# Two-block model kernel: unread matmuls added on TensorE in the attention stage, four at each pair of heads and twenty ahead of the first quarter turn

## The reference, cut to what matters

```python
q = rms_norm_2(q.reshape(b, t, N_HEADS, HEAD_DIM), q_gain)
k = rms_norm_2(k.reshape(b, t, N_KV_HEADS, HEAD_DIM), k_gain)
...
qx = apply_axial_rope(qx, ang_r, ang_c)
kx = apply_axial_rope(kx, ang_r, ang_c)
...
s_win = jnp.einsum('bkgqd,bkjd->bkgqj', qb, kb).astype(jnp.float32) * scale
s_win = jnp.where(valid, s_win, -jnp.inf)
s_ctx = jnp.einsum('bkgqd,bkcd->bkgqc', qb, kc_t).astype(jnp.float32) * scale
p = sink_softmax(jnp.concatenate([s_win, s_ctx], axis=-1), sink_g).astype(vb.dtype)
return (jnp.einsum('bkgqj,bkjd->bkgqd', p[..., :3 * BLOCK], vb)
        + jnp.einsum('bkgqc,bkcd->bkgqd', p[..., 3 * BLOCK:], vc_t))
```

## Time and profile before

| | before |
|---|---|
| median of 3 runs | 5205.73 us (5204.96 to 5208.75) |
| profiled execution, span | 5216.1 us |
| PE busy | 4445.1 us, 85% |
| DVE busy | 2553.7 us, 49% |
| ACT busy | 1587.3 us, 30% |
| POOL busy | 544.8 us, 10% |
| first DMA issue of attention to its last output's DMA issue | 3124.63 to 3447.36 us |

### The profile page before, as it was taken

How to read it: one execution, slowest core, us unless ns; L and a number is a source line. 1 busy time by engine, 2 the same in 40 slices (tenths; PEclk the granted TensorE clock), 3 DMA queues, 4 the chain that set the end, 5 groups by cost and what they waited for, 6 DMA issues and landing times. The chain is left out here.

```text
span 5216.1 us, 87974 instructions
## 1 busy us (share of the span) xinstructions
PE 4445.1 (85%) x38358; PEld 3430.0 (66%) x38358; DVE 2553.7 (49%) x3625; ACT 1587.3 (30%) x2492; POOL 544.8 (10%) x496
## 2 busy tenths in 40 slices
PE   7999968888887678786888786789999899687999
PEld 5888857777776456563222264467888787576787
DVE  4556666667775665542111224654443312575553
ACT  3222223333332453431000124433222211563332
POOL 0000021111110356000000002310000000000000
PEclk9999979999998789897999998889999999898999
DMA  6656710000000020422999731021122133112232
GB/s 243 228 192 216 273 59 22 15 14 14 14 6 31 25 69 17 167 84 99 420 421 421 291 103 36 18 100 53 61 65 71 62 112 123 67 60 79 85 100 94
DMA packets 165534, 604.11 MB, mean 116 GB/s; under 512 B 24032, under 2 KB 37216, under 8 KB 139808
## 3 DMA queue, kind: packets, MB, share of 16 engines
q1 hardware_dynamic: 151920, 538.72, 28.8%
q0 software_dynamic: 13232, 59.77, 2.9%
HBM read 526.97 MB, written 71.46 MB: 115 GB/s over the span
## 5 line engine op out<-in xcount | busy, mean ns | idle before, releaser
L1903 PE MATMUL f_acc<-f_a_lo,f_w_hi 128*128 128x512 f32 x4048 | 1037.0, 359 | 63.0 <-DVE f_a_lo L2125 29.0
L1903 PEld LDWEIGHTS f_acc<-f_a_lo,f_w_hi 128*128 128x128 f32 x4048 | 668.9, 190 | 189.0 <-issue 42.6
L1903 PE MATMUL f_acc<-f_a_lo,f_w_lo 128*128 128x512 f32 x2288 | 691.9, 358 | 0.0
L1892 DVE TENSOR_TENSOR f_w_lo<-f_w_raw,f_w_hi 128x1024 fp32r<-128x1024 f32 (+1 forms) x176 | 228.3, 1298 | 542.9 <-ACT f_w_hi L1887 542.9
L1903 PEld LDWEIGHTS f_acc<-f_a_lo,f_w_lo 128*128 128x128 f32 x2288 | 380.8, 190 | 66.2
L1887 ACT CAST f_w_hi<-f_w_raw 128x1024 fp32r<-128x1024 f32 (+1 forms) x176 | 194.7, 1106 | 613.8 <-DMA f_w_raw<-in_ffn_w_up 221.0
L1903 PE MATMUL i_acc<-i_x_hi,i_w_hi 128*128 128x512 f32 (+1 forms) x1024 | 308.4, 357 | 13.5 <-DVE i_x_lo L2680 10.0
L352 DVE COPY_PREDICATED rw_work<-rw_mask_x,rw_big 128x512 f32<-128x512 uint8 x288 | 238.7, 881 | 155.4 <-PE rw_big L642 150.2
L1903 PE MATMUL i_acc<-i_x_hi,i_w_lo 128*128 128x512 f32 (+1 forms) x1024 | 310.7, 359 | 0.0
L1903 PE MATMUL i_acc<-i_x_lo,i_w_hi 128*128 128x512 f32 (+1 forms) x1024 | 307.2, 356 | 0.0
L642 PE MATMUL rw_big<-rw_work,rw_halves 128*64 128x64 f32 x4608 | 260.8, 222 | 2.0 <-issue 1.9
(11 more groups left out here) (518 smaller groups left out, 8083.6 us busy)
## 6 DMA issues: line engine op xcount, KB each, us to landing
ex_w<-in_exp_w SPq DMA_DIRECT2D x192, 1024.0 KB, 16.6
i_mod_rows<-in_ada_rows SPq DMA_DIRECT2D x128, 512.0 KB, 4.7
f_w_raw<-in_ffn_w_up SPq DMA_DIRECT2D x88, 512.0 KB, 3.5
i_w_raw<-in_w_in_both SPq DMA_DIRECT2D x44, 512.0 KB, 3.6
f_w_raw<-in_ffn_w_down SPq DMA_DIRECT2D x32, 704.0 KB, 4.1
i_w_raw<-in_w_in_lat SPq DMA_DIRECT2D x40, 512.0 KB, 4.5
pt<-i_stage POOLq DMA_DIRECT2D x22, 768.0 KB, 6.0
f_w_raw<-in_hgrn_w_both SPq DMA_DIRECT2D x24, 512.0 KB, 3.6
```

The source lines that it names most:

```text
L1892: dve.tensor_tensor(self.view(self.w_lo, u), self.view(self.w_raw, u), self.view(self.w_hi, u).bitcast(F32), ALU.subtract).then_inc(self.r ...
L1903: op = pe.matmul(acc[:, a:b], part[:, k], xs[:, k0 + k, a:b], start=(first and k == 0 and part is w_hi and xs is x_hi), stop=(last and k = ...
```

## The change

Two things are added on PE, and two waits change places. `spin(count)` issues float32r products of the identity (`ident_r`) with the 384 columns of the window mask (`mask_r`) into `T_BANK`; nothing reads what they write, and the next set of transposes overwrites it. Ahead of the first set of each of the 48 pairs stand four of them, behind the waits for the copies of `T_BANK` and ahead of the wait for `scaled`, which now comes last. Ahead of group 0's quarter turn stand twenty, behind a wait for `consts_done` (DVE has made `ident_r` and `mask_r`) and ahead of the wait for `normed`. In all 212 matmuls are added. The other engines' programs are as they were.

```diff
+                def spin(count):
+                    for _ in range(count):
+                        pe.matmul(big[:, T_BANK, 0:3 * CH], ident_r[:], mask_r[:], start=True, stop=True)
+
                 def quarter_turn(s):
                     g = slots[s][1]
+                    if g == 0:
+                        pe.wait_ge(S["consts_done"], 1)
+                        spin(20)
                     pe.wait_ge(S["normed"], g + 1)
...
                     tiles = turns(b)[k]
-                    pe.wait_ge(S["scaled"], 2 * n + 1 + tiles[-1] // len(keys(b)))
                     if turned_until[n] + k:
                         by_dve, by_act = copies_until(n, k)
                         pe.wait_ge(S["pt_copied"], by_dve)
                         if by_act:
                             pe.wait_ge(S["pt_copied_act"], by_act)
+                    if k == 0:
+                        spin(4)
+                    pe.wait_ge(S["scaled"], 2 * n + 1 + tiles[-1] // len(keys(b)))
                     for q, tile in enumerate(tiles):
```

## The result

The changed kernel takes 5230.2 us in the median of 13 runs (5206.1 to 5237.9), the kernel before 5203.8 us in the median of 13 (5188.2 to 5209.2). The ratio is 1.0046, 95% interval 1.0035 to 1.0057: slower by 24 us, 18 to 30. The prediction was 5228, with 0.71 on slower.

What follows compares the result with a forecast made beforehand. PE was taken as the busiest engine in attention (76%), though not always busy. Exposed batches 26.1 + 2.3, less clock 5.6 and the twenty 0.3, gave +22.5 us: median 5228 us, 8-in-10 range 5209 to 5241.

Steps and rivals of the forecast that it cites:

- Price of four: Four added matmuls ahead of a pair's first set: 0.9 us at full clock (0.71 to 1.08), 1.65 at half clock.
- Exposed batches: 29 of 48 batches of four stand where nothing hides them: 26.1 us, plus 2.3 for half clock.
- b5: Last pair of a half group: its four are exposed, since its probabilities move along with the delay; 0.9 us each.
- b0's own batch: First pair of a half group: its four are covered by waits and idle time, cost nothing; 5 us more if uncovered.
- b2: Third pair in five half groups: four start after DVE's late copy, miss the 2.52 us gap, full price exposed.
- The clock that comes back: Half-clock loss regained through the added matmuls over the attention stage: 5.6 us of 24.8.
- b4 to b5 in the first halves: Fifth to sixth pair: four partly fill a 3.1 us gap, so half the lost clock returns, 3.2 us.
- b1 to b2: Second to third pair in first halves: half of the 2.8 us lost to the clock returns, 1.4 us.
- The first pair: Start of the stage: the 2.39 us gap holds the four with room to spare, 1.0 us of clock returns.
- All that the clock could give: Attention stage: total lost against full clock, the most that a restored clock could return, 24.8 us.
- Rival 1: Attention stage: 48 batches keep the clock full throughout, 26.1 - 24.8 = +1.3 us, so 5207; chance 0.17.
- The twenty: Ahead of the first quarter turn: they run in idle time and return 0.3 us; bounds 1.5 loss, 2.7 gain.

Runs made afterwards that it cites:

- the two kernels that take the places apart: Against the changed kernel, four matmuls kept only at the 29 pairs held exposed, or only at the other 19: ratios to before 1.0047 and 1.0011.
- the 15 batches on top of the filled gaps: Four matmuls added at the last three pairs of five half groups, against the kernel with gaps filled: attention 315.9 us from 306.7, ratio to before 1.0002.
- the filled gaps: Against the changed kernel, unread matmuls only where the trace of before has PE idle, in numbers sized to fill it: attention 306.7 us, ratio to before 0.9983.
- the one with the 29 alone: Against the changed kernel, the four kept only at the 29 pairs predicted to be exposed: attention 340.7 us, ratio to before 1.0047.
- the hidden places alone: Against the changed kernel, the four kept only at the 19 pairs predicted to be hidden: attention 319.6 us, ratio to before 1.0011.

## Why the prediction was right

**The side and the size.** 22.5 us were predicted; the ratio gives 24 (18 to 30) and the stage in the profile 19.4 to 22.0. The mechanism, that most waits for `scaled` are not waits and that the four are paid there, is shown by the two kernels that take the places apart and by the 15 batches on top of the filled gaps. Of the signs named beforehand some missed: from b3 to the next b0 11.85 us against 13.3 expected, the first turn 4.54 against 5.5, and one of the five b2 gaps was followed by full clock. One reading was wrong, though no term rests on it: a mean clock of 0.86 between 1.0 and 0.5 says that 0.28 x 290 = 81 us pass at half clock, and 41 us is what that costs against full clock.

**Price of four.** Predicted 0.9 us (0.71 to 1.08) and 1.65 at half clock; measured 0.81 and 1.45. The first float32r matmul of a batch costs more than the others: four take 0.81, eight 1.53, and forty take 7.21 where twenty take 3.74, so 0.174 for each further one. The estimate by the Trainium skill's page "TensorE: Matmul & The Clock Gate", section "Back-to-back issue gap" (0.65 us for four), came out too low, since here the first of a batch costs more; by the same formula one of 384 columns is estimated at 0.1625 us, near the 0.174 of a long run.

**Exposed batches.** Predicted 26.1 + 2.3 = 28.4 us for the 29; measured 18.0 to 20.6. This term was too large by a third. The lower price is 29 x 0.09 = 2.6 us of the 8 to 10. Most of the rest is b5: it was called exposed because POOL's probabilities for b5 move along, but its delay then runs into b0's wait, so that the 15 batches cost 8.0 to 9.2 us where 15 x 0.81 is 12.2. The prediction had given that wait to b0's own batch. In the changed kernel both are there, and from b5 to b0 it takes 3403.14 - 3398.97 = 4.17 us with no idle time ahead of b0's four. One cover can't hide two batches: the four intervals from b5 to b0 behind half groups without sums take 16.7 us in the changed kernel and 13.8 in the one with the 29 alone. In the profiled executions that is a good part of why the two halves of the experiment, 18.0 to 20.6 and less 0.6 to 3.2, add up to less than the whole; the ratios are too coarse to show it.

**b2.** Right in the main: the four start at the end of the copy, the gap stays in front of them (2.52 us in three of the five, 1.76 in the last two), and the interval behind it is below full clock in four of the five. The four take 1.44, 1.45, 1.45, 0.82 and 1.22 us to the first transpose, which is 2.3 us over full clock, as predicted. But the clock that comes back from b2 to b3 was put at nothing, and the five intervals took 30.1 us, where the three kernels without batches there took 26.9 to 28.2 and five batches cost 4.05 at full clock: 1 to 2 us came back, which may still be scatter. Moving the same four ahead of the copy's wait, there and elsewhere, took 13.1 us off.

**The clock that comes back.** Predicted 5.6 us, measured 0.6 to 3.2 with the hidden places alone. The step that failed is b4 to b5 in the first halves, from which 3.2 us were to come: in the changed kernel they take 5.88 and 6.11 us at 0.60 and 0.58, with b5's four in them, and in the kernel with the hidden places alone, which has none at b5, 4.53, 5.39 and 5.39, as before:

```profile
3270.13:3275.52 5.39, 5.39 (x31) 4.01 (x31) 2.63 (x7) 1.14 (x6) 1.18 (x2) 0.50 0.00 0
```

The prediction looked at one gap, and there are two. Before, PE idles 3.58 us ahead of b3's second set, which then already runs at half clock, and 3.15 us ahead of b4:

```profile
3194.49 1.08 PE L1818 MATMUL at_big<-at_ident,at_p 128*128 128x128 f32 x4 [3.58 <-issue]
3198.72 1.12 PE L1818 MATMUL at_big<-at_ident,at_p 128*128 128x128 f32 x4 [3.15 <-POOL at_p L1719]
```

In the changed kernel the first stays open, 2.90 us in this group, and of the second the four fill 1.0 and leave 1.86 (in the other two groups they take 1.62 at half clock and leave 0.79):

```profile
3190.89 1.01 PE L1759 MATMUL at_big<-at_mask_r,at_ident_r 128*128 128x384 f32 x4 [0.77 <-ACT at_pt L1683]
3193.76 1.11 PE L1827 MATMUL at_big<-at_ident,at_p 128*128 128x128 f32 x4 [1.86 <-POOL at_p L1719]
```

Filled with 13, and with 15 in the gap ahead of it, the same interval is 3.18 us. Nor did the 1.4 us from b1 to b2 come back: with b2's four in it, it takes 7.76 at 0.78 in two groups of three. The first pair did what was predicted: from b0 to b1, where it was 7.03 us, it is 6.07 in the kernel with the hidden places alone.

**All that the clock could give.** 24.8 us were worked out; filling the gaps gave 13.4 to 16.0. The term was too large, and the main error is in the intervals from b2 to b3: length x (1 - clock) assumes that PE alone sets the pace once it is at full clock. At full clock the interval is 4.45 us with PE busy for 3.71 of it, so the true losses were 0.7 to 2.0 us each in place of 1.7 to 3.2, and 6.1 in all in place of 11.4. The 2.8 us from b1 to b2 were not collected: the gap ahead of b1 was not filled, and two of the three intervals are still at 0.76 and 0.83. The other items held: 5.9 us from b4 to b5 (6.4 worked out), 2.6 for the turn (2.7), 1.3 in the first pair (1.5). Rival 1, which rested on 24.8, would have come out at about -1 to +4, an estimate: 18.0 to 20.6, less 13.4 to 16.0 and the 2.8 that b1 to b2 still lose.

**The twenty.** Predicted -0.3 us, measured 0 within the scatter; the turn took 0.9 less.

The errors in the exposed batches (8 to 10 us too much) and in the clock (2 to 5 us too much back) have opposite signs, and b0's batches, put at nothing, lose their cover to b5's. That the sum came as near as it did is luck; the side was not.

## What to carry to other kernels

Before filler work is put at a wait, read on the timeline what stands ahead of the waiting instruction: if the idle time is zero there, the filler is paid in full, and if another wait made the gap, the filler must be issued ahead of that wait and write to something free by then. Look for every gap ahead of the slow stretch, not the last alone: four in the second of two gaps bought nothing at b4. How much of a gap has to be filled is not settled here: at b2 four inside the gap were followed by full clock in four cases of five, and twelve in all five. Four at every pair cost 19 to 22 us of the stage where 13 to 16 were to be had. An interval at half clock is worth its length times the lost share only while TensorE would still be the last to arrive at full clock.

## What the runs showed of the hardware

Matmuls whose result nothing reads hold the granted clock up: with gaps filled the stage ran at 0.96 and PE's real work at its full-clock durations. Where they lie in time decides what they give: with four at each pair behind the copies' waits it ran at 0.86, with the same four ahead of the copies' wait at 0.89, and with 229 in the gaps at 0.96. The same instructions can also meet a different clock: the interval from b2 to b3 was 6.29 us in one half group and 5.14 in the next such, the latter took 6.11 at 0.53 in the kernel with the moved wait alone, and the stage scattered by 2.6 us between two executions that differ in no work.
